# Gate and up of a SwiGLU layer as a seven-product block product, with the product of silu and up and the activation's low part left on GpSimd

## The reference, cut to what matters

```
def swiglu_ffn(x, norm_g, w_gate, w_up, w_down):
    h = rms_norm(x, norm_g)
    return x + (jax.nn.silu(h @ w_gate) * (h @ w_up)) @ w_down

for i in range(2):
    x = ab_mixer(x, ...) if i % 2 == 0 else c_mixer(x, ...)   # both end in x + (...) @ w_out
    x = swiglu_ffn(x, ffn_norm[i], ffn_w_gate[i], ffn_w_up[i], ffn_w_down[i])
```

## Time and profile before

| | |
|---|---|
| median of three runs | 1798.6 us |
| profiled execution, first to last instruction (span) | 1794.4 us |
| instructions | 25153 |
| PE busy | 1737.0 us, 97% |
| DVE busy | 729.8 us, 41% |
| ACT busy | 550.5 us, 31% |
| POOL busy | 310.3 us, 17% |
| memory traffic | 104.20 MB, 58 GB/s |

### The profile page before, as it was taken

How to read it: one execution, slowest core, us unless ns; L and a number is a source line. 1 busy time by engine, 2 the same in 40 slices (tenths; PEclk the granted TensorE clock), 3 DMA queues, 4 the chain that set the end, 5 groups by cost and what they waited for, 6 DMA issues and landing times.

```text
span 1794.4 us, 25153 instructions
## 1 busy us (share of the span) xinstructions
PE 1737.0 (97%) x10092; PEld 1677.2 (93%) x10092; DVE 729.8 (41%) x822; ACT 550.5 (31%) x697; POOL 310.3 (17%) x167
## 2 busy tenths in 40 slices
PE   6999899999999999999999999899999999999998
PEld 5999789999999999999999777689999999999997
DVE  6432664333323333233443666643333233322333
ACT  4432343333411221122333566434332122211220
POOL 4000200221200221012223222122211012200210
PEclk8999999999999999999999999999999999999999
DMA  4222002212222222222121000022222222222113
GB/s 125 59 59 65 19 24 71 59 58 60 67 61 59 70 58 65 64 59 60 57 76 48 24 20 19 8 74 59 60 69 59 70 59 67 62 59 70 58 53 88
DMA packets 193594, 104.20 MB, mean 58 GB/s; under 512 B 3552, under 2 KB 190944, under 8 KB 193536
## 3 DMA queue, kind: packets, MB, share of 16 engines
q1 hardware_dynamic: 193056, 102.25, 19.5%
q0 software_dynamic: 144, 0.79, 0.1%
q10 hardware_dynamic: 336, 0.35, 0.1%
HBM read 100.23 MB, written 3.15 MB: 58 GB/s over the span
## 4 chain that ended last, share of the span: by engine, by line
PE 91%; DVE 4%; ACT 3%; issue 2%; POOL 1%; DMA 0%; DVEq 0%; ACTq 0%; SPq 0%; POOLq 0%
PE unit_ps L384 27%; PE unit_ps L386 27%; PE unit_ps L385 27%; PE unit_ps L714 2%; PE misc_ps L384 1%; PE misc_ps L386 1%; PE misc_ps L385 1%; PE misc_ps L513 1%; PE misc_ps L682 1%; PE misc_ps L499 1%; PE unit_ps L541 1%; DVE negmax L1349 0%; PE misc_ps L420 0%; ACT w_hi L800 0%; DMA x_tok<-in_x_sample 0%
## 5 line engine op out<-in xcount | busy, mean ns | idle before, releaser
L384 PE MATMUL unit_ps<-pair_a,w_hi 128*128 128x384 f32 x1872 | 633.9, 339 | 2.6 <-issue 1.4
L385 PE MATMUL unit_ps<-pair_a,w_hi 128*128 128x384 f32 x1872 | 626.3, 335 | 0.0
L386 PE MATMUL unit_ps<-pair_a,w_lo 128*128 128x384 f32 x1872 | 626.2, 335 | 0.0
L800 ACT ACTIVATE w_hi<-w_raw 128x1024 fp32r<-128x1024 f32 x190 | 201.5, 1061 | 902.1 <-PE unit_ps L386 889.5
L384 PEld LDWEIGHTS unit_ps<-pair_a,w_hi 128*128 128x128 f32 x1872 | 352.1, 188 | 7.1 <-issue 2.3
L385 PEld LDWEIGHTS unit_ps<-pair_a,w_hi 128*128 128x128 f32 x1872 | 352.2, 188 | 2.6
L386 PEld LDWEIGHTS unit_ps<-pair_a,w_lo 128*128 128x128 f32 x1872 | 352.0, 188 | 0.0
L1052 DVE TENSOR_TENSOR w_lo<-w_raw,w_hi 128x1024 fp32r<-128x1024 f32 x190 | 317.1, 1669 | 72.0 <-ACT w_hi L800 62.0
L384 PE MATMUL unit_ps<-pair_b,w_hi 128*128 128x384 f32 x960 | 323.5, 337 | 8.0 <-DVE x L1262 3.5
L386 PE MATMUL unit_ps<-pair_b,w_lo 128*128 128x384 f32 x960 | 321.2, 335 | 0.0
L385 PE MATMUL unit_ps<-pair_b,w_hi 128*128 128x384 f32 x960 | 321.2, 335 | 0.0
(11 more groups left out here) (185 smaller groups left out, 1224.1 us busy)
## 6 DMA issues: line engine op xcount, KB each, us to landing
w_raw<-in_w_gate SPq DMA_DIRECT2D x44, 512.0 KB, 3.8
w_raw<-in_w_up SPq DMA_DIRECT2D x44, 512.0 KB, 3.8
w_raw<-in_w_down SPq DMA_DIRECT2D x32, 512.0 KB, 3.8
w_raw<-in_ab_w_in SPq DMA_DIRECT2D x17, 512.0 KB, 3.9
w_raw<-in_w_down SPq DMA_DIRECT2D x16, 384.0 KB, 3.3
w_raw<-in_c_w_in SPq DMA_DIRECT2D x12, 512.0 KB, 3.7
w_raw<-in_ab_w_out SPq DMA_DIRECT2D x8, 512.0 KB, 3.8
w_raw<-const_dft SPq DMA_DIRECT2D x6, 512.0 KB, 3.2
```

The lines of the kernel that those rows point to most:

```text
L384: pe.matmul(out, w_hi, m_hi, start=start, stop=False)
L385: pe.matmul(out, w_hi, m_lo, start=False, stop=False)
L386: return pe.matmul(out, w_lo, m_hi, start=False, stop=stop)
L800: act.activation(whi[:, s, :, :], raw[:, s, :, :], ACT.Copy).then_inc(hi_split, 1)
```

## The change

The gate and up units of a hidden tile are no longer two units of 48 matmuls over the whole contraction. The contraction is halved (k tiles 0 to 3 and 4 to 7), which makes of gate two half tiles of weights G0 and G1, of up U0 and U1, and of `h` four blocks: H0a, H0b, H1a, H1b (half of the contraction, half of the tokens). The four results (gate and up, tokens a and b) then come from seven products of 12 matmuls each, in this order:

- P0: G0 by H0a
- P1: G1 by H1a
- P2: U0+U1+G0 by H0b-H1b-H0a
- P3: G0+U0 by H0b-H1b
- P4: U0+U1 by H0a-H0b
- P5: U1 by H1a+H0b-H1b-H0a
- P6: U0+U1+G0+G1 by H1b

P0, P2, P4 and P6 are added up in one PSUM bank (`xb`), P3 and P5 in another (`zb`), P1 has a third (`cb`). What stands in a bank between two products is needed by itself, so ACT copies it out on the way: after P0 (line 1189, semaphore `p1_kept`; PE's P2 waits for it), after P2 (line 1194, `u2_kept`; P4 waits) and after P3 (line 1200, `p7_kept`; P5 waits). DVE forms from these copies and the banks: gate of tokens a (line 1589), up of tokens b (line 1598, `c22_sum`; P6 waits), up of tokens a (line 1607). It scales gate by the inverse root mean square in two halves (lines 1609 and 1612); up isn't scaled, but the down units' results are (line 1569, new), before they are added to `x` (line 1572).

The weights of each product are a half tile of 128 x 512 with a high and a low part of their own: seven copies on ACT (line 989) and seven differences on DVE (line 1302) a pair, with four sums of weights on DVE ahead of them (lines 1311, 1313, 1316, 1321). There are four half slots for them, so the weights of a product four further on are prepared when a product has ended. Four raw slots take the place of two; the two new ones lie in the part of `pair_b` that chunks of at most 6 tiles leave free. The chunks become 4, 6, 6 and 6, so there are 8 down units more a layer, with the same matmuls in all.

The seven combinations of `h` with their high and low parts are made during the output projection ahead (`project`, instead of line 815's copy and line 1067's low part). All hardware loops of the feed-forward part are written out.

The core of the diff, PE and the pair's part of ACT, DVE and POOL:

```
-CHUNKS = (8, 8, 6)
+CHUNKS = (4, 6, 6, 6)
+PRODUCTS = 7
...
+            def product(n, combined, bank, starts):
+                half = HALF_AT[n]
+                pe.wait_ge(lo_split, n - KT + 1)
+                for k in range(HK):
...
+                    pe.matmul(out, hi, m_hi, start=starts and k == 0, stop=False, skip_group_check=True)
+                    pe.matmul(out, hi, m_lo, start=False, stop=False, skip_group_check=True)
+                    last = pe.matmul(out, lo, m_hi, start=False, stop=k == HK - 1, skip_group_check=True)
+                last.then_inc(unit_done, 1)
+            def pair_products(layer, q, n, after_units):
...
+                product(n, 0, xb, True)
+                if q:
+                    pe.wait_ge(c11_sum, q)
+                product(n + 1, 1, cb, True)
+                pe.wait_ge(p1_kept, q + 1)
+                product(n + 2, 3, xb, False)
...
+                product(n + 3, 4, zb, True)
...
+                pe.wait_ge(u2_kept, q + 1)
+                product(n + 4, 6, xb, False)
...
+                pe.wait_ge(p7_kept, q + 1)
+                product(n + 5, 5, zb, False)
+                pe.wait_ge(c22_sum, q + 1)
+                product(n + 6, 2, xb, False)
...
@@ ACT
+                        act.wait_ge(unit_done, n + 1)
...
+                        act.activation(T[2][:, 0:HALF], banks[:, xb, 0:HALF], ACT.Copy).then_inc(p1_kept, 1)
+                        ahead(n)
+                        ahead(n + 1)
...
+                        for j in (4, 5, 6):
+                            ahead(n + j)
+                        act.wait_ge(gate_scaled, 2 * (q + 1))
                         act.activation(T[0][:, :], T[0][:, :], ACT.Silu).then_inc(silu_done, 1)
-                        ahead_loop(n0, 1, i)
-                        act.wait_ge(prod_done, done + 1 + i)
+                        act.wait_ge(prod_done, q + 1)
                         act.activation(acts[:, i, 0, :], T[1][:, :], ACT.Copy).then_inc(act_hi, 1)
@@ DVE, down units
+                    dve.tensor_tensor(two(T[1][:, :]), down_banks(layer, f), rstd[:, :, :], ALU.mult).then_inc(
+                        y_scaled, 1)
+                    dve.wait_ge(y_scaled, KT * (len(CHUNKS) * layer + c) + f + 1)
+                    dve.tensor_tensor(x[:, f, :], x[:, f, :], T[1][:, :], ALU.add).then_inc(unit_read, 1)
@@ POOL
-                    with pool.Fori(0, tiles) as i:
-                        pool.wait_ge(silu_done, done + 1 + i)
-                        pool.wait_ge(unit_read, reads(n0 + 1) + 2 * i)
+                    for i in range(tiles):
+                        q = done + i
+                        pool.wait_ge(silu_done, q + 1)
+                        pool.wait_ge(c21_sum, q + 1)
+                        pool.wait_ge(c22_sum, q + 1)
                         pool.tensor_tensor(T[1][:, :], T[0][:, :], T[1][:, :], ALU.mult).then_inc(prod_done, 1)
```

In `project`, the work on one of the last four tiles (f from 4 on; T[0] and T[1] are two tiles of `h`, `hpair` holds the combinations), ACT's list:

```
+                    act.wait_ge(hp_lo, parts + KT + 4 * k)
+                    gained(layer, k, T[0])
...
+                    gained(layer, f, T[1])
...
+                    part_hi(1, f, T[1][:, 0:HALF])
...
+                    act.activation(hpair[:, 3:5, k, 0, :], nsum[:, :, :], ACT.Copy).then_inc(hp_hi, 1)
...
+                    squared(layer, f)
...
+                    part_hi(5, f, T[3][:, 0:HALF])
+                    part_hi(2, f, T[1][:, HALF:])
```

More of the change, by code:

```diff
@@ L147 @@
 SLOTS = max(max(PLAN), 8 * len(C_UNITS)) + 1
+FREE_SLOT = [1 - (BASE[f"gate_up{_l}0"] - 1) % 2 for _l in range(2)]
+assert all(t % 2 == 0 for t in CHUNKS)
 def broadcasts(g):
@@ L254, in trunk_kernel @@
         rope_landed = sem("rope_landed")
[L255 removed]
+        weights_landed = [sem(f"weights_landed{j}") for j in range(4)]
         hi_split, lo_split = sem("hi_split"), sem("lo_split")
@@ L630, in out_projection @@
             def out_projection(seg, pair, ready, count, kt, first=0):
-                n0 = BASE[seg]
-                with pe.Fori(first, KT // 2) as i:
-                    for s in range(2):
-                        linear(n0 + s + 2 * i, (n0 + s) % 2, pair, kt, (ready, count, reads(n0 + s - 2) + 2 * i))
-            def ffn(layer, g, r, pair, acts):
+                for j in range(2 * first, KT):
+                    n = BASE[seg] + j
+                    linear(n, n % 2, pair, kt, (ready, count, reads(n - 2)))
@@ L638, in ffn @@
+            def ffn(layer, pair):
                 done = FT * layer
@@ L640, in ffn @@
                     n0 = BASE[f"gate_up{layer}{c}"]
-                    def gate_up(i, first=False):
-                        for s in range(2):
-                            linear(n0 + s + 2 * i, (n0 + s) % 2, pair, KT,
-                                   (h_lo, KT * (r + 1), reads(n0 + s - 2) + 2 * i),
-                                   (lambda: trunk_sums(g, r)) if first and s == 0 else None)
-                            if s == 0 and first:
-                                broadcast(g)
-                    gate_up(0, c == 0)
@@ L651, in ffn, with after_units @@
-                    with pe.Fori(1, tiles) as i:
-                        gate_up(i)
-                    done += tiles
-                    out_projection(f"down{layer}{c}", acts, act_lo, done, tiles)
+                    units = KT * (len(CHUNKS) * layer + c)
+                    def after_units(which):
+                        if c == 0:
+                            pe.wait_ge(unit_read, reads(n0 - 2 + which))
+                        else:
+                            pe.wait_ge(y_scaled, units - 1 + which)
@@ L967, in _ @@
-            ffn(0, CHAIN["ffn0"], pairB, (2, "c", pairA))
+                    out_projection(f"down{layer}{c}", *(nxt if c == len(CHUNKS) - 1 and nxt else ()))
+            project("ab_out", 0)
+            ffn(0, pairB, (2, "c", pairA))
             def head_evacuate(i, n):
```

513 lines of the change are left out of this document (371 added, 142 removed).

## The result

The changed kernel took 1815.93 us in the median (1813.40 to 1816.39, 4 runs), the kernel before 1798.90 (1797.87 to 1802.17, 4 runs): ratio 1.0090, 95% interval 1.0076 to 1.0104. It is slower by 17 us; 1807 was forecast, 9 us less than was measured.

What follows compares the result with a forecast made beforehand. PE bounds the kernel before (97% busy, 16.64 us a pair); afterwards a ring of engines was to take 16.12. 1794.4 + 5.6 + 1.3 + 1.9 = 1803.2, with 4.2 offset 1807; range 1768 to 1850, own case 1800 to 1820.

Steps and rivals of the forecast that it cites:

- The ring: Steady gate/up pairs: engines waiting on each other take 16.12 us against 14.56 of matmuls; PE stands 1.56 at P2.
- The tail: In a pair, from DVE's line 1612 through silu, product, high and low part: 5.69 us, DVE starting at 5.56.
- One sign: In a pair of the changed kernel, DVE would be busy 11 to 12 us.
- Chunk ends: First down unit after a chunk grows by 2.0 us three times and 4.1 once: 10.1 a layer.
- A layer's start: First pair 24.7 us: PE waits 5.1 for the last tile's first part, then 4.8 for ACT's first copy.
- the second pair: The layer's second pair, taken as half-way to the ring: 15.7 us.
- The rival of the falling clock: PE's standing in pairs drops the clock to 1.2 GHz: pairs 29.1 us, kernel some 2250; chance 0.02.
- The output projection after attention: Its first three short units, already waiting for weights' low parts, get the longer chain: +1.3 us.
- The offset of 4.2: Us by which the median of the runs lies above the profiled execution, added to 1803.2 to give 1807.
- PE stays the bound: Rival, steady pairs: SBUF differences near 0.486 us, pairs 14.7, kernel 1756; decides at 0.53 an instruction; chance 0.24.
- No overlap at joins: Rival: back-to-back instructions on DVE and ACT don't overlap; pairs 17.0 us, kernel 1850; chance 0.26.
- the hold: A DVE instruction with two SBUF operands stands still while POOL works, starting 0.13 us before POOL's recorded end.

Runs made afterwards that it cites:

- the added matmul: One 384-column matmul, result overwritten, in front of each attention head's wait: 1805.24 us on the changed kernel, 1794.46 us on the kernel before.
- two lines of order on ACT: Changed kernel with ACT's first-bank copy and its copy of the fifth product's weights moved ahead of the activation's high part: 1762.17 us.
- taking GpSimd out: Changed kernel with the silu-and-up product and the activation's low part moved from GpSimd to DVE: 1762.90 us, ratio 0.9806.

## Why the prediction was right or wrong

The mechanism was right, and the number is 9 us low because the sum put at nothing the fall of the clock behind PE's longer waits (2.27 to 4.05 us, though not behind each of them). From the rows I estimate some 9 us for it outside attention (1.4 and 2.0 at the two starts, 1.4 in layer 1's second pair, 1.5 at each chunk of four, 1.5 in the output projection after attention). That the miss is no larger is in part luck, as the sum at the end of these terms shows.

**The ring: right.** 16.12 us forecast, 16.09 measured. The tail from the end of line 1612 to DVE's free run is 692.60 - 687.02 = 5.58 (forecast 5.56; 692.60 is 691.75 + 1.54 less 0.69), the rest 10.51 (8.54 + 2.02); differences take 0.68 to 0.69, waits 0.76, 0.37 and 0.44 where 0.80, 0.48 and 0.41 stood. One sign failed: DVE is busy 10.43 us in a pair, not 11 to 12. The prediction made ACT's copy the reason for which PE stands. Moving it was worth 0.8 of the 1.53 us, the two instructions behind the low part the other 0.7: PE's releaser is only the last link, and the sum, which went through DVE, was the better account.

**Chunk ends: the waits right, the clock left out.** 2.0 and 4.1 forecast; waits of 3.72 at the chunks of four and (17.4 - 2 x 3.72) / 6 = 1.66 at the others, and 0.30 for starting again. Behind the 3.72 come the 1.5 us of matmuls at half the clock, in each layer, which the forecast didn't have.

**A layer's start: right in place, mis-sized by some 3 us.** The waits were 4.73 and 4.05 (5.1 and 4.8 forecast). The pieces listed for a tile of `project` add up to 10.9 us, not to the 9.9 that the forecast went on with; measured are 8.94, 9.88 and 10.85, on the average 9.9. The term that failed is the second pair, "15.7, half-way to the ring". From the first pair's third product to the second's I had 4.16 + 10.64 + 1.1 = 15.9, with 2.5 for the column sums and the broadcast (left out on both sides, both inside these pairs) 18.4; measured 393.06 - 371.90 = 21.16. In it are nine matmuls at half the clock (1.44), and a ring that was not half-way but worse than steady: a wait of 2.27 instead of 1.23, which fits the table load of 1.28 in front of the silu (no run takes that load away). In layer 1 it was 1272.84 - 1251.00 = 21.84, and the third pair was late by 1.4 as well, after the clock fell again. With the chunk of four these make up the layers' 3.2 and 5.1 us above the forecast.

**Attention: not in the sum.** The rival of the falling clock was weighed for the pairs, where it stayed at 1.00, with 0.95 in attention, "with more idle", as the reason against it. That reading was wrong twice. Attention has less idle, 6.46 of 140 us, where the pair was to have 1.56 of 16.12. And 0.95 is an average: in the kernel before the clock is 0.57 from 1005 to 1013 and 0.66 from 1117 to 1127, around two slow bursts, and 1.00 in the rest of that stretch. The fall came in attention itself, where the stretch took 3.8 us more than forecast, 3.4 of which the added matmul takes away, and behind the longer waits elsewhere. The Trainium skill, "TensorE: Matmul & The Clock Gate", section "A second HAM failure mode: psum-queue depth-cycling", says that micro-idles between groups of matmuls throw the clock to and fro; the rows of attention now agree, those of the steady pair, which idles 1.23 us each time, do not.

**The projection in front of layer 0: overlooked, -4.3.** In the kernel before, the hardware loop reckons which add PE waits for from one start value (`reads(n0 + s - 2)`), and the units in front of the loop are not counted in it. So at each of its three turns PE waits for DVE's add of the unit just ended, not of the one before:

```profile
PE unit_ps L384 <- DVE x L1262: 3.5, 3, 1.2
```

Written out, these waits don't occur. **The output projection after attention**, +1.3 forecast, was +2.9: a wait of 2.87 where 1.65 stood, which is the 1.2, and behind it the matmuls at half the clock, some 1.5. **The offset of 4.2** between profile and median was 2.1 here: a run's time lies about 2 us above its own span, and the other 2 fit what the result section says of the span of before. **Up to the projection's first unit**, +1.6 stays unexplained.

Together: 1807 + 3.2 + 5.1 (layers) + 3.8 (attention) + 1.6 (output projection after it) - 4.3 (projection in front of layer 0) - 0.5 (end) + 1.6 (up to that projection) - 2.1 (offset) = 1815. The terms above the forecast come to 15.3 us, those below it to 6.9, and none of the latter was foreseen.

**Rivals.** PE stays the bound: refuted, the two-operand differences take 0.69 (under 0.53 would have been needed). No overlap at joins: refuted, 694.28 comes 0.08 before the end of 693.68 + 0.68. The Trainium skill, "VectorE: DVE Perf Modes", section "The DRAIN you can't avoid", has a first clause by which the next op waits for an empty pipe; these rows go by its second. And the hold: the Trainium skill, "SBUF — State Buffer", section "SBUF: two separate sides", calls the ports that DVE and GpSimd share an exclusive lock for a whole instruction; 1.54, 1.47 and 1.92 us instead of 0.69 agree. So it isn't semaphores alone that tie the engines together, as "The kernel before" has it.

## What to carry to other kernels

When work moves from PE to engines that wait for each other, go round the ring and write down what stands behind each instruction that another engine holds: two lines of order on ACT were worth 54 us here, as much as taking GpSimd out (53, of which some 8 are bursts in attention at the full clock). An average clock over a stretch hides where it falls; look at the bursts behind waits one by one. A loss of one per cent can contain a part, here about a fifth, in a stage that the change doesn't touch.

## What was not expected of the hardware

Identical bursts behind identical waits of 0.88 us run at clock 1.00 in one kernel, while in another the clock is 0.50 for their first 2 us, in head after head (3.70 and 5.20 us). One matmul in the wait leaves one slow burst of eight in the changed kernel (seven without it) and two of eight in the kernel before (three without it). What decides between the two when the wait is left alone stays open: the kernel before has both in one execution, and in the output projection the same wait (2.87 and 2.86 us) is followed by 0.50 in the changed kernel and by 1.00 in the changed kernel with the added matmul. And a wait of PE costs about 0.30 us more than the idle time that its row shows: 16.09 = 14.56 + 1.23 + 0.30, and 15.16 = 14.56 + 0.30 + 0.30. Of this, 0.16 is the overlap of rows (0.33 long, 0.17 apart) that falls away, and some 0.11 the slower start of the first matmul, behind which the next begins after 0.28.
